# Inverse roots of a head's norms by Ln and Exp at the joint between pairs, in a pooling / RWKV-7 decoder step

## What is computed

```python
wlog = -softplus(-(w0 + tanh(xw @ w1) @ w2)) - 0.5
decay = exp(-exp(wlog))
a = sigmoid(a0 + (xa @ a1) @ a2)
g = sigmoid(xg @ g1) @ g2
kk = heads(k * rwkv_kk)
kk = kk / maximum(sqrt(sum(kk * kk, axis=-1, keepdims=True)), 1e-12)
k = k * (1.0 + (a - 1.0) * rwkv_ka)
S, y = wkv7_scan(S0, r, decay, k, v, -kk, kk * a)      # per head, 64 x 64 state
yn = (y - mean(y)) * rsqrt(var(y) + GN_EPS)             # per head
out = ((yn * lnw + lnb + bonus) * g) @ wo
```

## Time and profile before

| | us |
|---|---|
| median of 3 runs (2903.09 to 2904.33) | 2903.64 |
| the profiled execution | 2906.42 |
| its span | 2904.6 |
| PE busy in the span | 2665.3 (92%) |
| DVE busy | 1641.6 (57%) |
| ACT busy | 1351.4 (47%) |
| POOL busy | 427.1 (15%) |

### The profile page before, as it was taken

One profiled execution on the slowest core, in us unless ns is written; L12 is line 12 of the kernel. 1 busy time (PEld: TensorE's weight loads), 2 busy tenths in 40 slices (PEclk: granted clock), 3 DMA queues, 4 the chain that ended last, 5 costly groups with the idle time before them and its releaser, 6 DMA issues.

```text
span 2904.6 us, 68158 instructions
## 1 busy us (share of the span) xinstructions
PE 2665.3 (92%) x25416; PEld 2558.3 (88%) x25416; DVE 1641.6 (57%) x2457; ACT 1351.4 (47%) x2301; POOL 427.1 (15%) x806
## 2 busy tenths in 40 slices
PE   3799999999999699998878888879899999999997
PEld 2799999999999699997666666669899999999997
DVE  6665545564565686434565655544666446554554
ACT  1477535553454364333444444433577435543552
POOL 4211001110012200000011111122121001100112
PEclk7899999999999899999999999989999999999999
DMA  3545444445444444443000000024454544454444
GB/s 111 160 153 162 157 159 152 162 149 166 158 153 141 152 160 154 158 161 103 14 25 25 25 25 25 30 104 161 140 166 158 171 163 161 163 166 166 159 147 143
DMA packets 113712, 378.14 MB, mean 130 GB/s; under 512 B 12080, under 2 KB 22960, under 8 KB 113328
## 3 DMA queue, kind: packets, MB, share of 16 engines
q1 hardware_dynamic: 113584, 376.26, 39.4%
HBM read 363.61 MB, written 12.60 MB: 130 GB/s over the span
## 4 chain that ended last, share of the span: by engine, by line
PE 87%; DVE 7%; ACT 3%; issue 2%; POOL 0%; DMA 0%; DVEq 0%; ACTq 0%; POOLq 0%
PE bank L542 25%; PE bank L544 25%; PE bank L543 24%; PE bank L650 11%; PE bank L620 1%; DVE ysd L1268 1%; DVE pext L1337 1%; DVE tb L1245 1%; ACT L991 1%; PE bank L781 0%; PE bank L784 0%; PE bank L831 0%; PE bank L604 0%; DVE rnorm L1127 0%; PE bank L832 0%
## 5 line engine op out<-in xcount | busy, mean ns | idle before, releaser
L1120 DVE TENSOR_TENSOR wlo<-raw,whi 128x1024 fp32r<-128x1024 f32 (+1 forms) x672 | 794.2, 1196 | 779.5 <-ACT whi L854 778.0
L542 PE MATMUL bank<-h_hi,whi 128*128 128x290 f32 (+1 forms) x3520 | 1060.0, 301 | 45.5 <-DVE h_lo L1146 38.3
L854 ACT ACTIVATE whi<-raw 128x1024 fp32r<-128x1024 f32 (+1 forms) x672 | 685.4, 1032 | 838.9 <-PE bank L544 816.6
L544 PE MATMUL bank<-h_hi,wlo 128*128 128x290 f32 (+1 forms) x3520 | 1057.8, 301 | 0.0
L543 PE MATMUL bank<-h_lo,whi 128*128 128x290 f32 (+1 forms) x3520 | 1056.8, 300 | 0.0
L542 PEld LDWEIGHTS bank<-h_hi,whi 128*128 128x128 f32 x3520 | 669.0, 190 | 49.3 <-issue 43.8
L543 PEld LDWEIGHTS bank<-h_lo,whi 128*128 128x128 f32 x3520 | 669.5, 190 | 0.0
L544 PEld LDWEIGHTS bank<-h_hi,wlo 128*128 128x128 f32 x3520 | 669.2, 190 | 0.0
L542 PE MATMUL bank<-act_hi,whi 128*128 128x304 f32 (+1 forms) x1376 | 410.1, 298 | 1.1 <-DVE act_lo L1205 1.1
L544 PE MATMUL bank<-act_hi,wlo 128*128 128x304 f32 (+1 forms) x1376 | 410.4, 298 | 0.0
L543 PE MATMUL bank<-act_lo,whi 128*128 128x304 f32 (+1 forms) x1376 | 409.7, 298 | 0.0
(11 more groups left out here) (209 smaller groups left out, 2937.5 us busy)
## 6 DMA issues: line engine op xcount, KB each, us to landing
raw<-W_all SPq DMA_DIRECT2D x648, 512.0 KB, 3.3
raw<-W_all SPq DMA_DIRECT2D x32, 192.0 KB, 3.1
wkv_out<-sout SPq DMA_DIRECT2D x16, 288.0 KB, 2.2
l<-L_all SPq DMA_DIRECT2D x16, 256.0 KB, 2.7
s<-wkv_st SPq DMA_DIRECT2D x16, 256.0 KB, 3.1
x<-xT SPq DMA_DIRECT2D x4, 608.0 KB, 5.8
x_spill<-x SPq DMA_DIRECT2D x1, 2432.0 KB, 7.2
x<-x_spill SPq DMA_DIRECT2D x1, 2432.0 KB, 9.9
```

Source lines behind the costliest of these rows:

```text
L542: mm_(acc, wh, xh, start=first, stop=False)
L544: return mm_(acc, wl, xh, start=False, stop=last)
L854: activation(WHI[q][:, 0:n], RAW[q][:, 0:n], ACT.Copy).then_inc(whi_ready, 1)
L1120: tt(WLO[q][:, 0:n], RAW[q][:, 0:n], WHI[q][:, 0:n].bitcast(f32), ALU.subtract).then_inc(wlo_ready, 1)
```

## The change

- The key norm of pair n is no longer Sqrt, max and reciprocal, but max with 1e-24 (DVE, from PSUM bank 4), then Ln and Exp(-0.5 x) on ACT. The deviation is Ln(var/64 + eps) straight from PSUM and Exp(-0.5 x). Both pairs of functions stand in the joint.
- The key norm is made one pair earlier, in the joint of the pair before: Square (ACT), head sums (PE, into bank 4), max (DVE), Ln, Exp. `pipeline` begins with t = -2 for it.
- The decay product moves from step 1 to step 0, the product for a from step 2 to step 1. Tanh of the decay stands at step 0, its Exp at step 1, Tanh of a at step 2, the scale of a at step 3.
- The scale of the finished pair moves on ACT from step 0 to step 4, before the copy of Y; POOL's two products of `finish` wait for it.
- DVE: the key vector NKK at step 0, the scan at step 2 ahead of SS, the reciprocal of PPT in two halves (steps 2 and 3), the b rows at step 3, the AR products before KR and TB. The product of KP and k moves from DVE to POOL.
- PE: from step 1 on, `early_products` stands ahead of the second `t1_products`.

```diff
 GN_EPS = 64e-5
 LORA = 96
-RSTEPS = 8
+NORM_FLOOR = 1e-24
+LN_SCALE = 65536.0
+RSTEPS = 5
 DECAY_SCALE = -float(np.exp(-0.5))
...
+        iteration(FIRST_STAGE, 0, operands=False, inverse=False, chain=False, finish=False)
         iteration(-1, 1, inverse=False, chain=False, finish=False)
...
                 def update_products(l, z):
-                    if l == 0:
-                        pe.wait_ge(*((tok_act, t + 1) if z else (stk_ready, t + 1)))
+                    if l == 0 and z == 0:
+                        pe.wait_ge(stk_ready, t + 1)
+                        pe.wait_ge(kkmax_ready, made(t + 2))
+                    elif l == 0:
+                        pe.wait_ge(tok_act, t + 1)
                     pe.wait_ge(t1_ready, 2 * LV * t + 2 * l + z + 1)
                     cs = level_chunks(l, z)
...
                     if chain:
                         rows_of_state(s_)
+                    if chain and s_:
+                        early_products(s_)
                     if inverse:
                         t1_products(s_, 1)
-                    if chain:
+                    if chain and s_ == 0:
                         early_products(s_)
...
                             pe.wait_ge(gg_ready, n)
-                        pe.wait_ge(kksq_ready, n + 1)
-                        head_sums(bank[7], TB).then_inc(kksum_mm, 1)
+                        pe.wait_ge(l2_loaded[m], by_parity(n, m))
+                        mm_(bank[7][:, 0:TOK], L2[m][:, 0:128], hidden[:, 0, :], start=True, stop=True).then_inc(z_mm, 1)
                     if chain:
...
                     if inverse:
...
                     if chain:
...
                     if operands and s_ == 1:
-                        pe.wait_ge(kkroot, n + 1)
-                        pe.wait_ge(l2_loaded[m], by_parity(n, m))
-                        mm_(bank[7][:, 0:TOK], L2[m][:, 0:128], hidden[:, 0, :], start=True, stop=True).then_inc(z_mm, 1)
-                    if operands and s_ == 2:
-                        pe.wait_ge(gates_ready, n + 1)
+                        pe.wait_ge(z_left, n + 1)
                         mm_(bank[7][:, 0:TOK], L2[m][:, 128:256], hidden[:, 1, :], start=True, stop=True).then_inc(lora_mm, 1)
...
                         update_products(s_, 1)
...
                     pe.wait_ge(rkk_ready, n + 1)
...
                 if chain:
-                    pe.wait_ge(*((kp_ready, n + 1) if operands else (gg_ready, PAIRS)))
+                    pe.wait_ge(*((ta_ready, n + 1) if operands else (gg_ready, PAIRS)))
                     pe.wait_ge(y_ready, j + 1)
                     head_sums(bank[7], YY[m]).then_inc(mean_mm, 1)
+                if ahead(t):
+                    if operands:
+                        pe.wait_ge(stk_ready, n + 1)
+                    pe.wait_ge(kksq_ready, n + 2)
+                    head_sums(bank[4], TB).then_inc(kksum_mm, 1)
                 if operands:
...
                         pe.wait_ge(vx_ready, j + 1)
...
                     pe.wait_ge(bonus_ready, n + 1)
...
                     turned(bank[6], KR).then_inc(trans_bk_mm, 1)
-                    pe.wait_ge(*((var_ready, j + 1) if chain else (kp_ready, n + 1)))
+                    pe.wait_ge(*((var_ready, j + 1) if chain else (ta_ready, n + 1)))
                     mm_(bank[7][:, 0:TOK], L2[m][:, 256:384], hidden[:, 2, :], start=True, stop=False)
...
             pe.wait_ge(b_free, G["o"] - 2)
-            for t in range(-1, PAIRS + 2):
-                iteration(t, t % 2, operands=t < PAIRS - 1, inverse=0 <= t < PAIRS, chain=1 <= t <= PAIRS, finish=t >= 2)
+            for t in range(FIRST_STAGE, PAIRS + 2):
+                iteration(t, t % 2, operands=-1 <= t < PAIRS - 1, inverse=0 <= t < PAIRS, chain=1 <= t <= PAIRS, finish=t >= 2)
             run("o", HHI1, HLO1, (h_ready, H_BEFORE["o"]))
...
                                bank[4 + z][:, C * k * w:2 * C * k].rearrange("p (w c t) -> p w c t", w=2 - w, c=k), ACT.Copy)\
                         .then_inc(xset_ready[z], 1)
-                if operands:
-                    if later(n):
-                        act.wait_ge(bonus_mm, n)
-                    activation(TB[:, 0:TOK], k_all[:, n, :], ACT.Square, scale=par("kk", n)).then_inc(kksq_ready, 1)
                 for s_ in range(LV):
...
                     if chain and s_ == 0:
...
                     if inverse:
...
                         x_evac(s_, 1)
-                    if finish and s_ == 0:
+                    if finish and s_ == 4:
                         act.wait_ge(scaled, t - 1)
...
                     if operands and s_ == 0:
-                        act.wait_ge(kksum_mm, n + 1)
-                        activation(TC[:, 0:TOK], bank[7][:, 0:TOK], ACT.Sqrt).then_inc(kkroot, 1)
+                        act.wait_ge(z_mm, n + 1)
+                        activation(DEC[:, 0:TOK], bank[7][:, 0:TOK], ACT.Tanh, bias=w0_half[:, ds(n)], scale=0.5).then_inc(z_left, 1)
                     if operands and s_ == 1:
-                        act.wait_ge(z_mm, n + 1)
-                        steps.done(activation(DEC[:, 0:TOK], bank[7][:, 0:TOK], ACT.Tanh, bias=w0_half[:, ds(n)], scale=0.5))
-                        steps.wait()
+                        act.wait_ge(z_left, n + 1)
                         activation(DEC[:, 0:TOK], DEC[:, 0:TOK], ACT.Exp, scale=0.5 * DECAY_SCALE, bias=decay_bias)\
...
                         act.wait_ge(lora_mm, n + 1)
-                        steps.done(activation(TA[:, 0:TOK], bank[7][:, 0:TOK], ACT.Tanh, bias=a0_half[:, ds(n)], scale=0.5))
-                        steps.wait()
+                        activation(TA[:, 0:TOK], bank[7][:, 0:TOK], ACT.Tanh, bias=a0_half[:, ds(n)], scale=0.5).then_inc(ta_ready, 1)
+                    if operands and s_ == 3:
+                        act.wait_ge(ta_ready, n + 1)
                         activation(KP[:, 0:TOK], TA[:, 0:TOK], ACT.Identity, scale=ka_half[:, ds(n)], bias=ka_rest[:, ds(n)])\
-                            .then_inc(kp_ready, 1)
+                            .then_inc(kr_ready, 1)
                     if chain and s_ == CHUNKS - 1:
-                        if finish:
-                            act.wait_ge(out_ready, t - 1)
+                        act.wait_ge(*((at_ready, t + 1) if inverse else (out_ready, t - 2)))
                         act.wait_ge(y_mm, j + 1)
                         activation(YY[m], bank[0][:, 0:TOK], ACT.Copy).then_inc(y_ready, 1)
+                if ahead(t):
+                    if operands:
+                        act.wait_ge(bonus_mm, n + 1)
+                    act.sem_inc(act_gate, 1)
+                    activation(TB[:, 0:TOK], k_all[:, n + 1, :], ACT.Square, scale=par("kk", n + 1)).then_inc(kksq_ready, 1)
                 if operands:
...
                     act.wait_ge(centered, j + 1)
                     activation(SQ, YY[m], ACT.Square).then_inc(ycsq_ready, 1)
+                if ahead(t):
+                    act.wait_ge(kkmax_ready, n + 2)
+                    steps.done(activation(TC[:, 0:TOK], TC[:, 0:TOK], ACT.Ln, scale=LN_SCALE))
+                if chain:
+                    act.wait_ge(var_mm, j + 1)
+                    activation(SD, bank[7][:, 0:TOK], ACT.Ln, scale=1.0 / HS, bias=GN_EPS).then_inc(var_ready, 1)
+                if ahead(t):
+                    steps.wait()
+                    activation(TC[:, 0:TOK], TC[:, 0:TOK], ACT.Exp, scale=-0.5, bias=0.5 * math.log(LN_SCALE))\
+                        .then_inc(kkroot, 1)
+                if chain:
                     act.wait_ge(var_ready, j + 1)
-                    activation(SD, SD, ACT.Sqrt).then_inc(gnroot, 1)
+                    activation(SD, SD, ACT.Exp, scale=-0.5).then_inc(gnroot, 1)
                 if operands:
                     act.wait_ge(gate_mm, n + 1)
...
                 def norms():
                     vec.wait_ge(kkroot, n + 1)
-                    link(ts(TC[:, T], TC[:, T], 1e-12, None, ALU.max))
-                    link(nc.vector.reciprocal(TC[:, T], TC[:, T]))
                     stt(NKK[:, T], k_all[:, n, :], kk_neg[:, ds(n)], TC[:, T], ALU.mult, ALU.mult)
                 def decays():
...
                     if later(n):
...
                     link(nc.vector.tensor_tensor_scan(PPT[:, T], ZD, DEC[:, T], 0.0, ALU.max, ALU.mult))
-                    nc.vector.reciprocal(PIN[:, T], PPT[:, T])
-                def b_rows():
-                    vec.wait_ge(kp_ready, n + 1)
-                    tt(KP[:, T], KP[:, T], k_all[:, n, :], ALU.mult)
-                    link(stt(TA[:, T], TA[:, T], 1.0, NKK[:, T], ALU.add, ALU.mult))
-                    stt(BR, TA, -0.5, PIN, ALU.mult, ALU.mult)
-                def k_rows():
-                    tt(KR, KP, PIN, ALU.mult).then_inc(bd_ready, 1)
-                    stt(TB[:, T], r_all[:, n, :], par("rk", n), KP[:, T], ALU.mult, ALU.mult).then_inc(rkk_ready, 1)
-                steps_n = {1: norms, 2: decays, 3: b_rows, 4: k_rows}
+                def inverses(lo, hi):
```

(32 more changed lines are left out.)

9 lines of the change are left out of this document (5 added, 4 removed).

## The result

The changed kernel takes 2853.56 us in the median of four runs (2851.12 to 2855.54), the kernel before 2903.36 beside it: a ratio of 0.9826, interval 0.9814 to 0.9839. The gain is 50 us where 67 were forecast. The time lies in the forecast range and 16.6 above the predicted number. The profiled execution took 2853.11, its span 2851.3. That is 53.3 less than the profiled execution before, and 51.3 of it lie in the recurrence, 581.6 to 530.3 when both are cut at ACT's first squares (1352.55, now 1350.66) and at its first reading of the result (1934.17, now 1880.96). The rest of the program moved by 2.0, 1.9 of them ahead of the recurrence.

A forecast was written before the change was run, and what follows sets the result against it. Mostly TensorE streaming weights, untouched; in the recurrence no engine is full and waits decide. Twelve steady pairs save 4.4 us each (53), the ends 14, together 67: 2837 us median, range 2813 to 2862.

The forecast's parts named there:

- Steps 0 to 3: Distances between the five state products of a steady pair: 5.03, 5.80, 4.65, 2.66 us before; 3.0, 3.85, 3.1, 2.85 forecast.
- Step 4 to Gram: Last state product to the Gram matrices: from 3.28 to 2.4 us, bounds 1.75 and 2.4, DVE waiting for POOL's product.
- Start, the wait for L2: Pair start to first state product: from 2.55 to 2.75, plus 0.9 us of PE waiting for the L2 weights.
- Joint, 10.9: Gram matrices to next pair's start: from 9.36 to 10.9 us (+1.5), as added head sums make everything behind them slide.
- so they start at 4.3: In the joint, head sums wait for DVE's copy of the KR Gram matrices, starting 4.3 us after Gram.
- The clock: Steady pairs: PE's granted clock below full adds 0.8 us a pair, half of 1.63, as PE's long idle gaps shorten.
- Together 14: Pipeline ends: t = 1 gains 4.5 us, t = 14 5.5, t = 15 to 17 4, t = -2 to 0 nothing; 14 in all.
- covered by 2.5: POOL's sax behind the finish products ends 3.5 us after Gram; PE wants it near 6, so 2.5 to spare.
- B: Rival, chance 0.13: DVE and POOL hinder each other everywhere from step 3 into the joint, 18 us more, 2855.
- C: Rival, chance 0.07: both ACT table changes in the joint cost their 1.28 load again while the engine empties; 22 more, 2859.
- D: Rival, chance 0.03: PE's clock drops in the unbroken run over joint and pair start, making the kernel slower, 2930.
- E: Rival, chance 0.08: ACT's chores cost as much in new places; only two reciprocals and one Sqrt won, 3 a pair, 2865.

## Why the prediction was right, and where it was wrong

- **Steps 0 to 3**: 12.68 measured, 12.8 forecast, in a pair at full clock. Counting what ACT does between the second `x_evac` and RHS was the right way; the scale put back gave 0.54 of step 0, the reciprocal put back 1.28 of step 1.
- **Step 4 to Gram**: 2.37 against 2.4. The upper bound was taken for DVE and POOL excluding each other, and four runs bear it out.
- **Start, the wait for L2**: 3.81 against 3.65 in this pair, 3.62 to 4.87 in the twelve, since the transfers took 2.5 to 3.8. Right in kind, 0.33 too small in the mean (3.98).
- **Joint, 10.9**: it is 11.29. The step that was 0.4 off is "so they start at 4.3": POOL's sax, late behind the finish products, holds the addition of the unit matrix for 0.32 (0.81 instead of 0.49), the copy of the Gram matrices comes that much later, and the head sums start at 4.62. I had seen such a hold and counted it in the 2.4, where it is not.
- **The clock**: 0.8 forecast over a pair at full clock. The mean pair is 0.72 above it, but 0.17 of that is the later L2, so the clock has about 0.55. I had taken half of 1.63 as a guess between two bounds, so that it came near is partly luck. The direction is right: the granted clock of the twelve went from 0.94 to 0.97. That the gaps are the reason is shown by the later runs alone.
- These make 30.87 against 30.55, 4 of the missing 16 us.
- **The step that failed is "Together 14"**, the ends, which brought 2.2. Pair by pair:
 - t = -2 to 0 were put at 0 and cost 3.5. Most of it is in the joint of t = 0. There the AR products take 0.85 beside KP*k and 1.42 beside the copies `vx`, which follow KP*k at once on POOL. PE waits 2.38 instead of 1.44, and then Gram and the bonus sums run at half clock; the new head sums come on top, with a wait of 0.82 for ACT's squares:

```profile
1389.41 2.40 PE L660 MATMUL bank<-ar,b_rows 64*64 64x128 f32 x20 [2.38 <-DVE k_rows L1308]
1391.57 2.38 PE L660 MATMUL bank<-ar,k_rows 64*64 64x128 f32 x20
1393.70 1.26 PE L660 MATMUL bank<-tb,ones 64*64 64x304 f32 x4
```

 - t = 14 brought 4.1 instead of 5.5, with a start of 4.68 behind a late transfer and a step 0 of 4.27, part of it at half clock.
 - t = 1 brought 1.15 instead of 4.5. It has no finish products, so sax follows KP*k at once and meets AR, as in the run with sax first: 3.23 to Gram instead of 2.37, and a joint of 13.03, part of it at half clock. Its start is 3.88 for another reason than in the steady pairs: PE waits 0.95 for ACT's s0a, behind the two table loads, and the early L2 load left it at 3.89.
 - t = 15 brought 0.1 and t = 16 to the end 0.4, together 0.5 instead of 4. The steps of t = 15 did shorten by 2.6, but sax stands behind the finish products there, and the joint has none of the other work that covers it: 7.55 instead of 4.98. I had checked that cover ("covered by 2.5") for a steady pair alone. With sax first in these pairs it is 5.53.

That the time lies in the range is owed in part to its width: its upper end of 2862, past B and C, leaves 25 us above 2837, and the ends alone took 12 of them.

The rivals: B gave 2855, nearly the measured time, and its mechanism is at work, but for 0.3 to 0.4 a pair beyond the forecast and in the ends, not for 1.35 everywhere. C is refuted (0.02 behind a load), D did not come, E neither (the steps are 3.02, 3.83, 3.02). But the run with four loads shows how near it was: two more loads undo the whole change, through a wait of PE and its clock.

## What to carry to other kernels

Work out the ends of a software pipeline stage by stage: a wait that is covered in the steady state is bare where its neighbours are missing. Where a DVE operation reads both operands from SBUF beside a POOL operation that reads SBUF, cost the two as one engine, and put POOL's work where DVE is idle. A wait of a microsecond or two on PE cost more than its length in these runs, because part of the work behind it ran at half clock: taking away 17.5 us of waits for L2 gave 24, taking away 1.19 in 13 joints (15) gave 20, and adding 2.52 in 13 joints (33) cost 66, though the waits for L2 went away there. So take away PE's waits first, by earlier loads and by other work put into them.

## What was not expected of the hardware

- The half-clock stretches follow waits, but not each: in the changed kernel the Gram matrices behind the same wait of 1.14 take 1.31 in one pair and 2.22 in the next. Removing another wait (for L2, some 16 us earlier in the same pair) or putting an unread product in this one made them rare or none. With a wait of 1.14 there, between none and seven of the twelve joints had such a stretch, by the run; with 1.02, where DVE makes KP*k, none of 24 had, and with 0.43 or less none of 36. What exactly decides is open.
- POOL's operations are stretched beside DVE's as well: yy 1.10 instead of 0.83, sax 1.38 instead of 1.15.
- A DVE operation that takes one operand from PSUM was not stretched: the first Gram copy of 128x512 (L1316) took 0.68 beside sax, as the second (L1320) did with POOL idle, while the addition behind it, with both operands in SBUF, went from 0.49 to 0.81.
- Even the two small DVE copies of five and eight columns, which read one operand (L1305, both in 0.25 us), took 0.75 beside POOL's finish products.
